# A 60-column operand for the compression products, their order among the query and key products, and the bias table's transfers on the weight queue

## The reference, cut to what matters

```python
def compress(raw, pos, w1, w2):
    blocks = raw.reshape(B, S_pad, G, HEAD_DIM)[:, cmp_idx] + pos[:, None, :]
    blocks = blocks.transpose(0, 3, 1, 2, 4).reshape(B, G, n_cmp, NSA_CMP_BLOCK * HEAD_DIM)
    return jax.nn.silu(blocks @ w1) @ w2

k_cmp = compress(kc, cmp_pos_k, cmp_k_w1, cmp_k_w2)
v_cmp = compress(vc, cmp_pos_v, cmp_v_w1, cmp_v_w2)
...
s_cmp = (jnp.einsum('gjqd,gnd->gjqn', qn, k_cmp[b]).astype(f32) * scale
         + tb_nsa[:, :, rel_bucket(d_cmp)])
p_cmp = masked_softmax(s_cmp, (d_cmp >= 0)[None, None])
o_cmp = jnp.einsum('gjqn,gnd->gjqd', p_cmp, v_cmp[b])
```

## Time and profile before

| | us |
|---|---|
| median of 3 runs | 1186.72 |
| lowest, highest | 1185.88, 1189.43 |
| span of the profiled execution | 1183.5 |

### The profile page before, as it was taken

One profiled execution on the slowest core, in us unless ns is written; L12 is line 12 of the kernel. 1 busy time (PEld: TensorE's weight loads), 2 busy tenths in 40 slices (PEclk: granted clock), 3 DMA queues, 4 the chain that ended last, 5 costly groups with the idle time before them and its releaser, 6 DMA issues.

```text
span 1183.5 us, 18540 instructions
## 1 busy us (share of the span) xinstructions
PE 1169.2 (99%) x7440; PEld 1024.3 (87%) x7440; DVE 833.2 (70%) x1269; ACT 664.0 (56%) x1083; POOL 214.6 (18%) x286
## 2 busy tenths in 40 slices
PE   9999999999999999999999999999999999999997
PEld 8886788888898788888888888899998699888886
DVE  7878777766568687666567877547977777777753
ACT  6538666643443666665446555545665865655641
POOL 0106442110000341111101111110002921111100
PEclk9999999999999999999999999999999999999999
DMA  8891345555457234555554554564463123555551
GB/s 309 254 245 40 107 179 202 186 213 193 152 192 285 73 142 178 179 188 204 214 181 147 205 179 169 182 203 161 168 214 141 50 99 128 184 178 183 189 194 76
DMA packets 33654, 206.05 MB, mean 174 GB/s; under 512 B 3856, under 2 KB 6432, under 8 KB 11808
## 3 DMA queue, kind: packets, MB, share of 16 engines
q1 hardware_dynamic: 29840, 200.60, 47.2%
q10 hardware_dynamic: 3728, 4.26, 1.7%
HBM read 203.39 MB, written 1.46 MB: 173 GB/s over the span
## 4 chain that ended last, share of the span: by engine, by line
PE 90%; DVE 3%; ACT 2%; DMA 2%; POOL 1%; issue 1%; ACTq 0%; DVEq 0%; POOLq 0%; SPq 0%
PE ps L684 41%; PE ps L689 22%; PE ps L701 3%; PE ps L702 3%; PE ps L703 3%; PE ps L2059 2%; PE ps L2058 2%; PE ps L2057 2%; DMA raw<-wstream 1%; PE ps L1015 1%; PE ps L756 1%; PE ps L757 1%; PE ps L758 1%; DMA h<-xt 1%; DVE wl L632 1%; PE ps L715 1%
## 5 line engine op out<-in xcount | busy, mean ns | idle before, releaser
L632 DVE TENSOR_TENSOR wl<-raw,wh 128x2048 fp32r<-128x2048 f32 (+4 forms) x190 | 417.2, 2202 | 101.1 <-ACT wh L603 101.1
L603 ACT ACTIVATE wh<-raw 128x2048 fp32r<-128x2048 f32 (+2 forms) x192 | 350.9, 1831 | 126.7 <-PE ps L689 54.0
L684 PE MATMUL ps<-xb,wh 128*128 128x512 f32 x1392 | 333.6, 392 | 0.0
L684 PEld LDWEIGHTS ps<-xb,wh 128*128 128x128 f32 x1392 | 255.6, 188 | 51.0 <-issue 0.8
L684 PE MATMUL ps<-ab,wh 128*128 128x512 f32 x772 | 188.3, 392 | 0.6 <-DVE ab L1081 0.6
L689 PEld LDWEIGHTS ps<-xb,wl 128*128 128x128 f32 x1392 | 178.4, 191 | 6.8
L689 PE MATMUL ps<-xb,wl 128*128 128x256 f32 x1392 | 180.5, 283 | 0.0
L684 PEld LDWEIGHTS ps<-ab,wh 128*128 128x128 f32 x772 | 140.6, 188 | 28.2 <-DVE ab L1081 1.5
L940 DVE TENSOR_TENSOR tf<-ps,tf 128x256 f32<-128x256 f32 x148 | 62.3, 424 | 103.0 <-ACT tf L935 103.0
L935 ACT ACTIVATE tf<-ps 128x256 f32<-128x256 f32 x148 | 56.2, 382 | 121.0 <-PE ps L689 120.7
L689 PEld LDWEIGHTS ps<-ab,wl 128*128 128x128 f32 x772 | 101.1, 191 | 5.1
(11 more groups left out here) (371 smaller groups left out, 1720.2 us busy)
## 6 DMA issues: line engine op xcount, KB each, us to landing
raw<-wstream SPq DMA_DIRECT2D x168, 1024.0 KB, 4.8
raw<-wstream SPq DMA_DIRECT2D x16, 704.0 KB, 4.2
raw<-wstream SPq DMA_DIRECT2D x4, 792.0 KB, 4.2
raw<-wstream SPq DMA_DIRECT2D x4, 512.0 KB, 6.6
e_bt<-scratch ACTq DMA_DIRECT2D x16, 128.0 KB, 8.1
o_bt<-scratch SPq DMA_DIRECT2D x2, 1024.0 KB, 5.8
raw<-wstream SPq DMA_DIRECT2D x2, 560.0 KB, 8.6
raw<-wstream SPq DMA_DIRECT2D x2, 528.0 KB, 3.4
```

The lines of the kernel that those rows point to most:

```text
L603: e.g.activation(WH[i % HLN][:, 0:w], RAW[i % RAWN][:, 0:w], ACT.Copy).then_inc(S["hi"], 1)
L632: e.g.tensor_tensor(WL[q][:, 0:w], RAW[i % RAWN][:, 0:w], f32(WH[q][:, 0:w]), ALU.subtract).then_inc(S["lo"], 1)
L684: e.g.matmul(two(PS[p.bank[p.unit(n)]][:, :]), WH[c % HLN][:, at * 128:at * 128 + 128], x2[:, :, tile(ks[k])], start=k == 0, stop=False, s ...
```

## The change

- The two halves of the windows lie side by side in one tile, `e_blk` (for each row group 30 columns high, 30 low), so that one operand of 60 columns is loaded: two products for each row group, with wh and with wl, instead of three. The result has 60 rows; the upper and the lower 30 are added only afterwards. (That adds a low x low term to the sum.)
- ScalarE copies the 60 x 256 result out as it is. hs is now four products with `e_fold`, a 60 x 30 matrix of two unit matrices that GpSimd makes; it turns and adds at once. The sigmoid comes behind hs, on 128 x 120: one exponential, one addition, one reciprocal.
- The order is cmpk, qn, cmpv, ks, hs, then the first three eighths of ev0, kc, vc, and the rest of ev0; the weight stream is packed accordingly.
- The bias: VectorE copies the row ahead of the low half of km's first chunk. SP, not ScalarE, writes it to `scratch` behind the fetch of cmpk's second chunk, then fetches the four following chunks and issues two transfers of `e_bt` behind each; each transfer is for 16 partitions and all 16 heads (256 KB), eight in all.

The diff, without the list of semaphores, two waits on the renamed semaphore, and lines that only move with their neighbours:

```diff
@@ -60,9 +60,9 @@
 
     first = chunks[0]
     chunks[0] = [first[8 * n + k] for k in range(8) for n in range(2)]
-    for name in ("cmp_k_w1", "cmp_v_w1"):
-        toks(name, 0, 0, 256, range(16), 8)
+    toks("cmp_k_w1", 0, 0, 256, range(16), 8)
     cols("even_w_in", 0, [[(1536 + 64 * j, 64), (1536 + 64 * (4 + j), 64)] for j in range(4)], k8, 16)
+    toks("cmp_v_w1", 0, 0, 256, range(16), 8)
     cols("even_w_in", 0, [[(2304, 128)], [(2560, 128)]], k8, 16)
     toks("even_w_in", 0, 1024, 512, k8, 4)
     for half in range(2):
...
@@ -293,10 +293,11 @@
     return [
         Gemm("r", "cols", 2, 8, 16, "ev_dve", kmajor=2),
         Gemm("qm", "cols", 4, 8, 16, "ev_dve", wide=True), Gemm("km", "cols", 4, 8, 16, "ev_dve", fixed=(4,)),
-        Gemm("cmpk", "line", 1, 16, 8, "ev_dve"), Gemm("cmpv", "line", 1, 16, 8, "ev_dve"),
+        Gemm("cmpk", "line", 1, 16, 8, "ev_act"),
         Gemm("qn", "cols", 4, 8, 16, "ev_dve", wide=True),
+        Gemm("cmpv", "line", 1, 16, 8, "ev_act"),
+        Gemm("ks", "cols", 2, 8, 16, "ev_dve", fixed=(3, 4), wide=True),
         Gemm("hs", "small", 1, 0, 0, "ev_dve"),
-        Gemm("ks", "cols", 2, 8, 16, "ev_dve", fixed=(3, 4), wide=True),
         Gemm("kc", "small", 1, 0, 0, "ev_dve", fixed=(0,)), Gemm("vc", "small", 1, 0, 0, "ev_dve", fixed=(1,)),
         Gemm("ev0", "toks", 512, 8, 4, "ev_act", fixed=(6, 5)),
         Gemm("cs0", "small", 1, 0, 0, "ev_dve", ring=1), Gemm("cs1", "small", 1, 0, 0, "ev_dve"),
...
-        e_blkl = place("e_blkl", 2 * 480, F32R, at=rl)
+        e_fold = place("e_fold", 30, at=m)
+        e_blk = place("e_blk", 4 * 480, F32R, at=rl)
         e_hz = place("e_hz", 256, at=late)
         e_hs = [place("e_hs", 256, at=late), SMALL[:, 256:512]]
...
 
-        def spread_bias(e, half):
-
-
-            e.wait_ge(S["d_scr"], 16)
-            hs = slice(2048 * half, 2048 * half + 2048)
-            for a in range(8):
-                src = bass.AP(scratch.tensor, 8 * half * 16 * 385 + 127 - 16 * a, [[384, 16], [16 * 385, 8], [1, 256]])
-                e.g.dma_start(e_bt[16 * a:16 * a + 16, hs].rearrange("p (h s) -> p h s", h=8), src).then_inc(S[f"bt{half}"], 16)
+        def spread_bias(e, shares):
+            for a in shares:
+                src = bass.AP(scratch.tensor, 127 - 16 * a, [[384, 16], [16 * 385, 16], [1, 256]])
+                e.g.dma_start(e_bt[16 * a:16 * a + 16, :].rearrange("p (h s) -> p h s", h=16), src).then_inc(S["bt"], 16)
...
         def sp_even(e):
             sp_gemm(e, G["r"])
             sp_gemm(e, G["qm"])
             sp_gemm(e, G["km"])
-            for name in ("cmpk", "cmpv", "qn", "ks", "ev0"):
+            row = TMP[1][0:16, 0:384]
+            e.wait_ge(S["row"], 1)
+            e.g.dma_start(bass.AP(scratch.tensor, 0, [[16 * 385, 16], [385, 16], [1, 384]]),
+                          bass.AP(row.tensor, row.offset, [list(row.ap[0]), [0, 16], [1, 384]])).then_inc(S["d_scr"], 16)
+            for x in range(4):
+                fetch_to(e, G["km"].first + 4 + x)
+                if x == 0:
+                    e.wait_ge(S["d_scr"], 16)
+                spread_bias(e, (2 * x, 2 * x + 1))
+            for name in ("cmpk", "qn", "cmpv", "ks", "ev0"):
                 sp_gemm(e, G[name])
             sp_gemm(e, G["ev1"])
             sp_gemm(e, G["eo"])
 
...
         btv = e_bt[:, :].rearrange("p (h s) -> p h s", h=16)
 
...
+            ident = c_("ident")
+            e.g.tensor_tensor(e_fold[0:60, :], ident[0:60, 0:30], ident[0:60, 30:60], ALU.add).then_inc(S["fold"], 1)
             e.wait_ge(S["er"], 1)
             for i in range(2):
                 pos = v_("posk" if i == 0 else "posv")
                 for g in range(2):
-                    bv = blk[i][:, 0:480].rearrange("p (m n) -> p m n", m=16)[:, :, g * 15:g * 15 + 15]
+                    bv = windows(i)[:, :, g * 15:g * 15 + 15]
                     s = 2 * i + g
...
             for i in range(2):
-                sl = slice(i * 480, i * 480 + 480)
                 e.wait_ge(S["blk"], i + 1)
-                e.g.activation(e_blkh[:, sl], blk[i][:, 0:480], ACT.Copy).then_inc(S["blkh"], 1)
-            e.wait_ge(S["row"], 1)
-            row = TMP[1][0:16, 0:384]
-            e.g.dma_start(bass.AP(scratch.tensor, 0, [[16 * 385, 16], [385, 16], [1, 384]]),
-                          bass.AP(row.tensor, row.offset, [list(row.ap[0]), [0, 16], [1, 384]])).then_inc(S["d_scr"], 16)
+                e.g.activation(halves_of[:, i, :, 0, :], windows(i), ACT.Copy).then_inc(S["blkh"], 1)
             act_gemm(e, G["km"])
-            for i, name in enumerate(("cmpk", "cmpv")):
-                p = G[name]
-                act_gemm(e, p)
-                e.wait_ge(*p.end[0])
-                if i:
-                    e.wait(G["cmpk"].out[0])
-                e.g.activation(e_hz[0:30, :], PS[p.bank[0]][0:30, 0:256], ACT.Exp, scale=-1.0).then_inc(S["cz"], 1)
+
+            def hidden(i, p):
+                def drain(e, _):
+                    e.wait_ge(*p.end[0])
+                    e.g.activation(e_hs[i][0:60, :], PS[p.bank[0]][0:60, 0:256], ACT.Copy).then_inc(S["ev_act"], 1)
+                return drain
+
+            act_gemm(e, G["cmpk"], drain=hidden(0, G["cmpk"]))
             act_gemm(e, G["qn"])
-            spread_bias(e, 1)
-            act_gemm(e, G["ks"])
-            spread_bias(e, 0)
+            act_gemm(e, G["cmpv"], drain=hidden(1, G["cmpv"]))
+            act_gemm(e, G["ks"], ahead=1)
+            e.wait_ge(*G["hs"].end[0])
+            e.g.activation(e_hz[:, 0:120], PS[G["hs"].bank[0]][:, 0:120], ACT.Exp, scale=-1.0).then_inc(S["cz"], 1)
             act_gemm(e, G["ev0"], drain=act_toks(G["ev0"], e_v, 0, 0))
             for tb in range(2):
...
-
-            def table_row(e, c):
-                lo_to(e, G["km"].first + 1)
                 e.wait_ge(S["table"], 1)
                 e.g.tensor_copy(TMP[1][0:16, 0:384], PS[3][0:16, 0:384]).then_inc(S["row"], 1)
+                lo_to(e, G["km"].first)
 
             dve_gemm(e, G["r"], 0)
             dve_gemm(e, G["qm"], 1, first=first_norm, drain=dve_to(G["qm"], e_qm, 0, by=1),
-                     between=table_row)
+                     between=lambda e, c: lo_to(e, G["km"].first + 1))
             for i in range(2):
-                sl = slice(i * 480, i * 480 + 480)
                 e.wait_ge(S["blkh"], i + 1)
-                e.g.tensor_tensor(e_blkl[:, sl], blk[i][:, 0:480], f32(e_blkh[:, sl]), ALU.subtract).then_inc(S["blkl"], 1)
+                e.g.tensor_tensor(halves_of[:, i, :, 1, :], windows(i), f32(halves_of[:, i, :, 0, :]),
+                                  ALU.subtract).then_inc(S["blkl"], 1)
             lo_to(e, G["cmpk"].first + 1)
-            dve_gemm(e, G["km"], 1, drain=dve_to(G["km"], e_km, 0), between=lambda e, c: lo_to(e, G["cmpv"].first))
-            for i, name in enumerate(("cmpk", "cmpv")):
-                p = G[name]
-                dve_gemm(e, p, 0)
-                e.wait_ge(S["cz"], i + 1)
-                hz = e_hz[0:30, :]
-                e.link(e.g.tensor_scalar(hz, hz, 1.0, None, ALU.add))
-                e.settle()
-                e.link(e.g.reciprocal(hz, hz))
-                e.settle()
-                e.g.tensor_tensor(e_hs[i][0:30, :], PS[p.bank[0]][0:30, 0:256], hz, ALU.mult).then_inc(S["ev_dve"], 1)
+            dve_gemm(e, G["km"], 1, drain=dve_to(G["km"], e_km, 0), between=lambda e, c: lo_to(e, G["qn"].first))
+            dve_gemm(e, G["cmpk"], 0)
             dve_gemm(e, G["qn"], 0, drain=dve_to(G["qn"], e_qn, 0, by=1))
+            dve_gemm(e, G["cmpv"], 0)
+            dve_gemm(e, G["ks"], 0, drain=dve_to(G["ks"], e_ks, 0), ahead=1)
             p = G["hs"]
-            o = PS[p.bank[0]]
-            e.wait_ge(*p.end[0])
-            e.g.tensor_copy(e_ht[:, :], o[:, 0:60])
+            o, hz = PS[p.bank[0]], e_hz[:, 0:120]
+            e.wait_ge(S["cz"], 1)
+            e.link(e.g.tensor_scalar(hz, hz, 1.0, None, ALU.add))
+            e.settle()
+            e.link(e.g.reciprocal(hz, hz))
+            e.settle()
+            e.g.tensor_tensor(e_ht[:, :], o[:, 0:60], hz[:, 0:60], ALU.mult)
             e.wait_ge(S["zero"], 1)
             for jb in range(2):
                 for g in range(2):
-                    srcv = o[:, 64 + jb * 30 + g * 15:64 + jb * 30 + g * 15 + 15]
-                    ins = e.g.tensor_copy(hrv[:, jb, g, :, 0:15], srcv.unsqueeze(1).broadcast_to([128, 4, 15]))
+                    c = 60 + jb * 30 + g * 15
+                    ins = e.g.tensor_tensor(hrv[:, jb, g, :, 0:15], o[:, c:c + 15].unsqueeze(1).broadcast_to([128, 4, 15]),
+                                            hz[:, c:c + 15].unsqueeze(1).broadcast_to([128, 4, 15]), ALU.mult)
             ins.then_inc(S["ev_dve"], 1)
-            dve_gemm(e, G["ks"], 0, drain=dve_to(G["ks"], e_ks, 0))
+            lo_to(e, G["ev0"].first + 1)
             for name, dst, n in (("kc", e_kc, 15), ("vc", e_vc, 128)):
                 p = G[name]
```

(34 more changed lines are left out.)

## The result

The changed kernel takes 1198.87 us (median; 1191.5 to 1207.56) against 1186.65 us of the kernel before (1185.49 to 1189.43) on the same chip: a ratio of 1.0107, 95% interval 1.0083 to 1.0131. It is slower by 1.1%, above the upper end of the range. The profiled execution took 1196.13 us.

A forecast was written before the change was run, and what follows sets the result against it. Bound by weight transfers before ks, not TensorE: products -3.7 us and gap -1.35, but spreads idle TensorE some 6.5 us, so +0.9, plus hs 0.4: +1.3 on 1186.7, 1188.0 us. Forecast 1184.7 to 1191; whole range 1181 to 1196.

The forecast's parts named there:

- rival B: Early bias spreads on SP's queue run at the scratch write's pace, 5.2 us a pair: +10.1 us, 1196.8; chance 0.22.
- The path: From the compression products to ks, weight transfers rather than TensorE set the time; ks starts at about 64.2.
- c9 to c11: Weight chunks in stream order, here cmpv's two and ks's, behind spreads on SP's queue; 9 us and more to landing.
- The price of a pair of spreads, b: Time of two bias spreads, 0.52 MB, on SP's queue: taken as 3.0 us, range 2.6 to 3.3.
- The landing: SP's queue never runs dry from 35.7, so ks's chunk data end at 35.7 + 14.0 + 12.0 = 61.7.
- w: Transfer time of one 1.05 MB weight chunk on SP's queue: taken as 2.8 us, range 2.5 to 3.2.
- The clock: TensorE's granted clock, full after the 1.35 us pause; no row tells what a longer pause does.
- hs: Four fold-matrix products replacing four transposes, now behind ks: 0.4 to 0.55 us against 0.36, taken as +0.05.
- The compression: cmpk and cmpv on TensorE: the 60-column operand removes 32 of 96 products, 3.7 us.
- rival A: Early spreads don't hold up the weight chunks, full saving: -3.7 - 1.35 = -5.1 us, 1181.6; chance 0.26.
- The alternation: Order cmpk, qn, cmpv, ks lets chunks gather between short products; by itself it would remove the 1.35 us gap.
- What was put at nothing: Table-row copy on VectorE, GpSimd's fold addition, SP's waits, sigmoid and low half of ev0's second chunk: no time.

The follow-up runs named there:

- e7: Changed kernel with only the first four bias spreads early, the other four behind the fetch of c13 (ev0's second weight chunk): 1189.43 us, ratio 1.0028.
- e3: Changed kernel with each 256 KB bias spread sent as two halves of 128 KB, same place and queue: 1194.14 us, ratio 1.0067.
- e4: Changed kernel with each 256 KB bias spread written to every eighth partition instead of 16 neighbours, read step shifted to match: 1189.84 us, ratio 1.0033.
- e1: Changed kernel with its bias transfers put back where the kernel before has them, late on ScalarE's queue: 1182.31 us, ratio 0.9973.
- e11: Changed kernel with its eight 256 KB spreads to every eighth partition, behind the fetch of ev0's second weight chunk: 1181.56 us, ratio 0.9950.
- e13: e11 with the old order of products, cmpk, cmpv, qn, ks: 1184.09 us, ratio 0.9985.
- e12: Changed kernel with sixteen early spreads of 128 KB, each to every eighth partition: 1190.1 us, ratio 1.0032.
- e10: e8 with the scratch write back on ScalarE's queue, as in the kernel before: 1185.64 us, ratio 0.9981.
- e2: Kernel before with the early bias transfers alone; compression, order and sigmoid as before: 1201.14 us, ratio 1.0127.
- e8: Changed kernel with all spreads as sixteen halves on SP's queue behind the fetch of ev0's second weight chunk: 1184.74 us, ratio 0.9985.

## Why the prediction was wrong

The forecast was 1188.0 and the time 1198.9: rival B's case, 1196.8, and 2 us beyond it. The profiled execution, from which the terms below are read, took 1196.13, 2.7 us less than the median. Going by the prediction's own steps:

*The path.* Right. It said that the transfers and not TensorE set the start of ks, that the waits stand ahead of cmpv's halves, and that c9 to c11 land late. They took 14.7, 21.3 and 17.5 us, the first just short of the 15 us that it had named as the mark of B and the others past it. Only the wait ahead of ks isn't there: ks was held by c10, through cmpv's second half, and not by its own chunk.

*The price of a pair of spreads, b.* **This is the step that failed.** It was taken as 3.0 us, from 0.48 MB in 3 us and 0.20 in 1. But those rows are of spreads of 128 KB; the change sends 256 KB. The prediction noted that each new spread keeps the engines on one row of 16 partitions twice as long, and still kept its range for b to 2.6 to 3.3 and gave the slow rate to a rival with 0.22. e7 has the rate for the size that the change uses, 0.117 MB/us, so 4.5 us. Four pairs are 4 x 1.5 = 6.0 us. The far end, the scratch write with 5.2, was nearer than the middle. B had ks at 73.0 and it started at 72.86. That they meet is luck: B reached it with a b of 5.2, the run with 4.5, a late c10 and the clock. The Trainium skill's page "SBUF — State Buffer", section "Door 1: The DMA port swizzle", gives 104 GB/s for partitions 0 to 15. The whole spreads with 117 GB/s come near it, the halves with 138 to 180 don't; the prediction weighed the rule against rows of the other size, and let it fall for that.

*The landing.* With b = 4.5 and w = 2.8 the sum gives 35.7 + 14.0 + 18.0 = 67.7 for c11, 68.2 with the half microsecond; it landed at 69.58, 1.4 us later. c7 by the same sum is there at 39.0 and was at 39.3, c8 at 46.3 and was at 47.71, so the 1.4 us is there from c8 on. c10 by the same sum: 35.7 + 11.2 + 13.5 + 0.5 = 60.9, and it landed at 65.23, 4.3 us later. The sum serves one transfer after the other at one rate. In e3 and e4 too c10 comes late and c11 close behind it (8.2 and then 4.4 us; 7.4 and 5.5; in the change 9.7 and 4.35), so it isn't a chance of one execution; what holds c10 back is open. It made c10 the bound: 65.23, its low half from 67.17 to 69.46, then cmpv's 16 products. (The half microsecond to the semaphore stands in no row of before, and no run here measures it alone.)

*The clock.* Left as "no row tells". Those 16 products took 3.34 us instead of 1.85. Against c11's own high half, done at 71.5, c10's way costs 1.4 us more (72.86). Together 6.0 + 1.4 + 1.4 = 8.8: ks at 72.9 instead of the forecast's 64.1 to 64.2.

*hs.* Taken as 0.41 us; it took 1.00 (78.54 to 79.54): the trace has eight records for the four products with the fold matrix. 0.6 us of the total. From ks to the scores: 22.42 us, 21.23 before, +1.2 where +0.4 was said.

*The compression.* Right in direction, and nearly in size. Without the early spreads it was forecast at -5.1 us (rival A). The medians give -3.7 for e1 and -5.25 for e11 (1186.81 to 1181.56). In the traces, from cmpk's first product to the first scores, it is 45.43 us before, 42.50 in e1 and 41.04 in e11, so -2.9 and -4.4. The -4.4 is the forecast less the 0.64 us by which hs got dearer (1.00 against 0.36). e1 lacks another 1.5: 0.79 of a wait for the sigmoid, which the prediction had put at nothing and which isn't there in e11, 0.29 ahead of cmpv's second half, and 0.4 that isn't explained.

*The alternation.* Right: said to close the gap and let chunks gather; e13 against e11 shows 2.96 us in the trace and 2.5 in the medians.

*What was put at nothing.* The copy of the table's row, the fold addition on GpSimd, SP's waits: no wait in the profile after stands on any of them. The low half of c13 is hidden as said.

*The chances.* B had 0.22. Since 5w + 4b was known to decide from b = 3.6 on, and b had bounds of 2.6 and 5.2 with the untested doubling of the size in between, B deserved as much as the forecast.

*The sums.* Redone, the forecast's range runs from -1.8 to +4.5 us where it says -2 to +4.2, and TensorE's idle time is 6.3 us where it says 6.5. The measured time lies outside either way.

## What to carry to other kernels

Price a transfer by a row of the same size and the same partitions, and where the change alters one of them, treat the old rate as one end of the range and not its middle. A load that has slack is not free to move early: it takes the DMA engines' time from the weights whichever queue it is on, so put it behind the last weight chunk of the tight stage, and then look at who reads the next chunk after it. When a product gets cheaper than the load of its operand, order matters more than length: put a long product between two short ones.

## What the runs showed of the hardware

- A transfer of 256 KB from DRAM to 16 neighbouring partitions, in pieces of 1 KB, ran at 0.117 MB/us; halves of 128 KB at 0.138 and 0.18 in two executions, and 256 KB to every eighth partition, with another step of the reads, at 0.20. All at a share of 114 to 116% of the engines, so the share says nothing of the rate.
- Ahead of 59.90 TensorE had stood for 4.34 us, and its granted clock is 0.50 from 60 to 70, the 1.2 GHz level, through 16 products and another idle stretch; in 70 to 75 it is 0.73, and full after. In e12 a wait of 4.29 us has the same effect (4.71 us for 16 products of ks that take 3.83), and so have shorter ones: 3.06 us in e10, 2.90 in e4, 2.81 in e7, 2.19 in e2. In e7 a second wait of 2.18 us hasn't, nor have 0.81 and 2.04 us in e13. So the length of the wait doesn't decide alone. In e2:

```profile
46.87 0.39 PE L1469 MATMUL ps<-wh,e_blkh 128*30 128x256 f32 x1 [2.19 <-DVE wl L632]
47.06 0.41 PE L1470 MATMUL ps<-wh,e_blkl 128*30 128x256 f32 x1
47.27 0.41 PE L1471 MATMUL ps<-wl,e_blkh 128*30 128x256 f32 x1
```
- Four f32 products with the 60-row fold matrix leave eight records and take 1.00 us, 0.125 each for 30 columns.
- e8, in whose fastest execution c14 lands at 74.87, scatters by 7 us (1180.8 to 1187.6); e11, whose c14 lands at 72.86, keeps within 0.55.
